# A norm's bias in the last stage: the add moves from VectorE to GpSimd, behind the fetch of the tile three ahead

## The reference

```
ye = ye * gates.reshape(-1)[order][:, None]
y = jax.ops.segment_sum(ye, tok, num_segments=T)
x = layer_norm(DEEPNORM_ALPHA * x + (1.0 + g2[:, None]) * y, ln_g[i, 1], ln_b[i, 1])

def layer_norm(x, g, b):
    mu = jnp.mean(xf, -1, keepdims=True)
    var = jnp.mean(jnp.square(xf - mu), -1, keepdims=True)
    return ((xf - mu) * lax.rsqrt(var + LN_EPS) * g + b)
```

## Time and profile before

| | us |
|---|---|
| median of three runs | 3309.64 |
| lowest, highest | 3308.8, 3313.45 |
| span of the profiled execution | 3305.4 |

### The profile page before, as it was taken

How to read it: one execution, slowest core, us unless ns; L and a number is a source line. 1 busy time by engine, 2 the same in 40 slices (tenths; PEclk the granted TensorE clock), 3 DMA queues, 4 the chain that set the end, 5 groups by cost and what they waited for, 6 DMA issues and landing times. The chain is left out here.

```text
span 3305.4 us, 53689 instructions
## 1 busy us (share of the span) xinstructions
PE 2907.2 (88%) x18381; PEld 2560.3 (77%) x18381; DVE 2401.0 (73%) x3523; ACT 1367.5 (41%) x2036; POOL 1684.4 (51%) x1045
## 2 busy tenths in 40 slices
PE   7599999999999999999946999970999999999920
PEld 2399999999999999999933888850788888888820
DVE  3578888888888888888843333442888888888868
ACT  1333434333343434343311121110677777777733
POOL 0034444444344444444420222225799999999975
PEclk9799999999999999999968999985999999999965
DMA  6653533535343353533235223233987878767767
GB/s 249 279 192 132 173 132 116 179 129 175 134 175 133 110 195 109 189 144 122 97 143 192 96 107 109 102 115 95 364 317 286 286 286 302 269 234 275 271 224 246
DMA packets 255051, 618.33 MB, mean 187 GB/s; under 512 B 16742, under 2 KB 91242, under 8 KB 245610
## 3 DMA queue, kind: packets, MB, share of 16 engines
q1 hardware_dynamic: 209290, 505.15, 42.6%
q10 hardware_dynamic: 33120, 70.27, 5.6%
q0 software_dynamic: 12544, 41.97, 3.7%
HBM read 609.68 MB, written 99.93 MB: 215 GB/s over the span
## 5 line engine op out<-in xcount | busy, mean ns | idle before, releaser
L1441 DVE TENSOR_TENSOR piece_lo<-piece_raw,piece_hi 128x2048 fp32r<-128x2048 f32 x187 | 562.4, 3026 | 120.3 <-ACT piece_hi L1541 120.2
L1541 ACT CAST piece_hi<-piece_raw 128x2048 fp32r<-128x2048 f32 x280 | 525.8, 1909 | 236.6 <-issue 80.0
L1441 POOL TENSOR_TENSOR piece_lo<-piece_raw,piece_hi 128x2048 fp32r<-128x2048 f32 x93 | 569.5, 6124 | 22.4 <-ACT piece_hi L1541 20.3
L568 PE MATMUL pj<-hm,w_hi 128*128 128x256 f32 x4096 | 540.6, 285 | 34.8 <-DMA hm<-hm_parts 22.4
L568 PEld LDWEIGHTS pj<-hm,w_hi 128*128 128x128 f32 x4096 | 509.8, 192 | 37.9 <-DMA hm<-hm_parts 22.7
L523 POOL TENSOR_TENSOR xd<-y,xd 128x512 f32<-128x512 f32 x64 | 99.5, 1555 | 560.9 <-DVE y L840 560.9
L781 DVE SCALAR_TENSOR_TENSOR cv<-ub,parb,cv 128x256 f32<-128x256 f32 x768 | 333.4, 507 | 22.8 <-ACT cv L680 14.9
L568 PE MATMUL pj<-hm,w_lo 128*128 128x256 f32 x2048 | 287.7, 283 | 0.0
L581 PE MATMUL pj<-w_hi,hm 128*128 128x256 f32 x2048 | 281.6, 285 | 6.3 <-ACT cv L680 6.3
L568 PEld LDWEIGHTS pj<-hm,w_lo 128*128 128x128 f32 x2048 | 264.4, 192 | 0.0
L581 PEld LDWEIGHTS pj<-w_hi,hm 128*128 128x128 f32 x2048 | 258.3, 191 | 7.7 <-ACT cv L680 7.7
(11 more groups left out here) (285 smaller groups left out, 6969.4 us busy)
## 6 DMA issues: line engine op xcount, KB each, us to landing
hm<-hm_parts SPq DMA_DIRECT2D x64, 2048.0 KB, 7.8
piece_raw<-in_w_gate SPq DMA_DIRECT2D x94, 1024.0 KB
piece_raw<-in_w_up SPq DMA_DIRECT2D x94, 1024.0 KB
piece_raw<-in_w_down SPq DMA_DIRECT2D x92, 1024.0 KB
acb<-acum_rows SPq DMA_DIRECT2D x64, 512.0 KB, 3.6
expert_out<-ye ACTq DMA_DIRECT2D x46, 512.0 KB
hm_parts<-hl SPq DMA_DIRECT2D x8, 2048.0 KB, 13.3
w_raw<-in_w_in SPq DMA_DIRECT2D x32, 512.0 KB, 6.2
```

The costliest lines, as they stand in the source:

```text
L568: mm = nc.tensor.matmul(pj[m % 3][:, 0:CHUNK], wp[m][:, kk, :], hm[b][:, hp, kk, :], start=n == 0, stop=n == 3 * KK - 1)
L1441: v.tensor_tensor(lo[q][:], raw[q][:], hi[q][:].bitcast(F32), ALU.subtract).then_inc(lo_done[q], 1)
L1541: nc.scalar.copy(hi[q][:], raw[q][:]).then_inc(hi_done[q], 1)
```

## The change

VectorE no longer adds the bias. GpSimd does it, in place, in the same step i for tile i - 1, behind its fetch of tile i + 3; it waits for `og_done`, the multiply of that step, and counts `o_done` up, for which SyncE's store waits. Before its first fetch GpSimd now waits for both rows of the norm (`row_in`, 32). All else is as before, VectorE's own wait for `row_in` too.

```diff
@@ GpSimd, step(i, s)
                 if in_loop(i, 0, TT - R + 1):
                     fetch(i + R - 1, (s + R - 1) % R)
-
+                if in_loop(i, 1):
+                    ob = o[(s - 1) % 2]
+                    pool.wait_ge(og_done, i)
+                    nc.gpsimd.tensor_tensor(ob[:], ob[:], lnb[:], ALU.add).then_inc(o_done, 1)
+
+            pool.wait_ge(row_in, 32)
             for i in range(R - 1):
                 fetch(i, i)
@@ VectorE, step(i, s)
                     nc.vector.tensor_tensor(o[1 - b][:], r[1 - b][:], lng[:], ALU.mult).then_inc(og_done, 1)
-                    dve.wait_ge(og_done, i)
-                    nc.vector.tensor_tensor(o[1 - b][:], o[1 - b][:], lnb[:], ALU.add).then_inc(o_done, 1)
```

## The result

| | median us | lowest, highest | runs |
|---|---|---|---|
| before | 3311.55 | 3308.8, 3314.84 | 4 |
| with the change | 3339.88 | 3336.83, 3340.76 | 4 |

The changed kernel is slower: 28.3 us between the medians, the ratio is 1.0083 with a 95% interval of 1.0068 to 1.0097. 3337.8 us was forecast, from 3309.64 plus 28.2.

The account below looks back on a forecast made before the run. VectorE was taken as full, GpSimd nearly, its SBUF reads standing still behind VectorE's two-input instructions. Rounds 22.7, last tile 1.9, last add 1.3 and start 2.3 sum to 28.2 us on 3309.64: 3337.8 us, range 3330 to 3347.

Parts of the forecast that it names:

- 14 rounds, multiply to multiply: Output stage's loop, first to fifteenth multiply: each round grows from 6.84 to 8.46 us, 22.7 us in all.
- last tile's nmr: End of the stage: fifteenth tile's multiply to its successor's nmr grows from 2.40 to 4.29 us, +1.9.
- last add: End of the stage: last multiply's start to last add's end grows from 2.49 to 3.76 us, +1.3.
- start: Stage's start: GpSimd's row wait shifts the first fetch by up to 6.2 us; +2.3 reaches the first rstd's end.
- The circle: Each round: multiply, add on GpSimd, rstd, nmr, r, statistics, multiply wait on one another, 8.46 us long.
- A: Output stage: VectorE's L1754 (m) and GpSimd's add run one behind the other, +28.2 us; chance 0.76.
- B: Output stage: the add overlaps VectorE's L1754 (m), +23.4 us, 3333.0 us; chance 0.08.
- The size of a round: Loop round: 3.99 us from multiply's end to nmr, plus 4.47 to the next multiply's end, 8.46 us.
- One sign: Profile after, middle round: GpSimd's add row about 3.3 us long, 1.1 of it standing still.
- GpSimd's own queue: GpSimd's queue in a loop round: the fetch ends 0.38 us before the add could begin, costing nothing.
- E: Output loop: the fetch becomes the bound, 0.95 us more a round over 12 rounds, +11.4, 3349.2 us; chance 0.10.
- Rival C: Output loop: the add is hidden and VectorE's shorter queue sets the round, -14.0 us, 3295.6 us; chance 0.03.

Follow-up runs that it names:

- run 1: Changed kernel, GpSimd waiting for the norm rows only ahead of its first add, not its first fetch: stage 156.4 us, against 159.5 with the change.
- run 2: Kernel before, with only the wait for the norm rows put ahead of GpSimd's first fetch; VectorE still adds the bias: stage 135.7 us.
- run 3: Changed kernel with GpSimd adding only 256 of the 1024 bias columns: mean round 6.78 us from 8.40, stage 135.1 us.
- run 4: Changed kernel with VectorE's m operation cut to 8 of 1024 columns: stage 154.8 us, against 159.5 with the change.
- run 5: Changed kernel with GpSimd's add put ahead of the fetch of the same step: stage 203.8 us, against 159.5 with the change.
- run 8: Kernel before, statistics moved from VectorE to ScalarE, m with four buffers: 3301.78 us against 3309.12, ratio 0.9979; stage 123.4 us.
- run 7: Changed kernel with the add one step later, behind the fetch's copies and waiting for VectorE's r of the same step: stage 145.4 us.
- run 6: Changed kernel with the add one step later, between rstd and the fetch: 3333.15 us against 3309.76 for the kernel before, ratio 1.0064; stage 155.6 us.

## Why the prediction was right, point by point

| step | forecast us | measured us | shown by |
|---|---|---|---|
| 14 rounds, multiply to multiply | 14 x 1.62 = 22.7 | 117.55 - 95.25 = 22.3 | trace after |
| last tile's nmr | +1.9 | 4.18 - 2.40 = 1.8 | trace after |
| last add | +1.3 | 3.64 - 2.49 = 1.15 | trace after |
| start | +2.3 | 32.65 - 29.40 = 3.25 | trace after, runs 1 and 2 |
| sum | 28.2 | 28.5 | |

**The sum.** That 28.2 comes so near to 28.5 and to 28.3 is in part luck: the start was forecast 1 us too low, and the other three terms together 0.7 too high. The start's size is also one execution's (see below), and the 95% interval of the ratio spans 22.5 to 32.1 us. What was right is the mechanism and its price per round.

**The circle.** The path named (multiply, add behind m, rstd, nmr) is the one in the rows, and runs 3, 4 and 5 change it term by term: the add's duration counts in full, m in front of it counts 0.2 us with a fetch and 1 us without, and what stands between add and rstd counts in full. A, the forecast, is shown, and B's price as well: run 4 is nearly B, and at 154.8 it is 4.7 below the change, where the working of B had 4.8 less than A.

**The size of a round.** 8.40 against 8.46. The add ended 3.38 after the multiply where 3.46 was taken from L1063. From there to nmr's start were 0.56, where the working had 0.50 and 0.03. The rest of the round, 4.46, stayed as forecast (4.47). One sign was read wrong: in a middle round the add's row was to be 3.3 us long. It is 2.53 to 2.56, because the row begins only when yb is through, 0.83 after the multiply; 3.31 stands in the two rounds without a fetch. Its end, on which the sum rests, isn't touched by that.

**GpSimd's own queue.** yb was to end 0.38 us before the add could begin. It ends at 3241.92 in the round above, m at 3242.28: 0.36. E, the fetch as the bound, needed 0.59 us more of fetch, and did not come. Two rounds of the loop, the first of each turn, are 0.1 longer (8.53); there the copy gb and not ga was held by r, and the fetch ran that much later.

**The start** is the term that was mis-sized, by 1 us. The shift of the first copy was right, 6.24 (13.44 less 7.20) against 6.2. What was wrong is how much of it the first rstd's slack takes up. I had let the last fetch get shorter by 0.4, since its yb might no longer wait for VectorE. It didn't (0.94 against 1.75), but the ya ahead of it stood behind VectorE's second m (1.74 in place of 0.96), and an earlier ya had to wait too (1.35), so the four fetches took 15.45 us in place of 15.07. Run 2 shows that the term also depends on when the row lands, so that 3.25 is one execution's value.

**The ends** were sized 0.1 too high each: the add without company took 2.34, not 2.39, and came 0.07 after the multiply's end, not 0.15.

**Rival C, faster.** It needed an add that ends less than 0.64 us behind m. Run 3 is near that point: its add ends 0.59 behind m (3244.12 against 3243.53), and the mean round is 6.78, against 6.80 before. By the Trainium skill's Perfetto Trace Analysis, section Optimizing Scalar/DVE Operations, giving work of a saturated VectorE to ScalarE or even GpSimd may make sense, but between VectorE and GpSimd it might not help, because they share a read port. The runs agree: with ScalarE's passes the stage was 7.6 us under the kernel before (run 8), with the add on GpSimd 14.4 us over it at best (run 7). Not all of that is the port. In the change itself run 4 puts the standing behind m at 4.7 of the 28.5 us; the larger part is the add's own duration in the circle (run 3).

What stays open: the bias row landed 5.7 to 7.2 us after its issue in the ten profiles, and nothing was tried on why.

## What to carry to other kernels

Before an operation goes to an idle-looking engine, write down what is queued behind it there and who waits for that: here GpSimd's busy share of the stretch hardly moved (63.29 to 65.65 of 76 us), and the add cost 1.6 us a tile because the next tile's rstd stood behind it. On GpSimd, ask also what VectorE does at that moment: in these runs GpSimd's add and a VectorE instruction with two inputs in SBUF didn't run side by side, and the second of the two stood still, even at 128x1 (2.30 us in place of 0.16). Where VectorE is full and ScalarE idle, look at ScalarE too: here it took over the statistics, which have one input, and the stage fell by 7.6 us.

## What the runs showed of the hardware

A VectorE instruction with two SBUF inputs on one element a partition (nmr) took 2.30 us in place of 0.16 behind a GpSimd add of 128x1024; the statistics with one input lost nothing beside the same add (1.29 us alone and beside). That it goes this way too, and costs the shortest instruction the whole of the other's duration, I had not put into the expectation of run 6. The Trainium skill's SBUF — State Buffer, section Who interferes with whom, calls the port pair that VectorE and GpSimd share an exclusive lock, says that a VectorE instruction with two SBUF inputs contends with a GpSimd instruction that reads SBUF, and that the order of issue decides which of them blocks. The rows of runs 4 and 6 agree, with GpSimd second in the change (add 3.31 us, 2.34 in run 4) and VectorE second in run 6. GpSimd's float32 add took 2.34 us for 1024 columns and 0.72 for 256, with VectorE idle.
